# A bidirectional encoder block on one core: VectorE's order of work inside the RWKV-7 scan is changed

## The reference, cut to what matters

```python
k_dir = to_heads(k_raw[None] * (1.0 + (iclr - 1.0) * k_a[layer]))
wkv = rwkv7_bidir_scan(dir_stack(r_h, r_h), dir_stack(decay_h[0], decay_h[1]),
                       dir_stack(k_dir[0], k_dir[1]), dir_stack(v_h, v_h),
                       dir_stack(kk, kk), dir_stack(iclr_h[0], iclr_h[1]))
...
bonus = jnp.sum(jnp.sum(r_h[None] * k_dir * r_k[layer], axis=-1, keepdims=True) * v_h[None], axis=0)
o_rwkv = (gn + bonus.reshape(b, s, RWKV_WIDTH)) * gate
...
gates = jax.nn.sigmoid(z_gate.astype(f32).reshape(b, s, N_BRANCHES, D_MODEL) + b_gate[layer])
```

## Time and profile before

| | |
|---|---|
| median of 3 runs | 3952.27 us (3950.05 to 3955.77) |
| profiled execution | 3961.35 us, its span 3959.6 us |
| TensorE busy over the span | 3582.5 us (90%) |
| VectorE busy | 1654.8 us (42%) |
| scan, first `n_sb` to last | 1227.50 to 1979.56 us from the span's start |

### The profile page before, as it was taken

One profiled execution on the slowest core, in us unless ns is written; L12 is line 12 of the kernel. 1 busy time (PEld: TensorE's weight loads), 2 busy tenths in 40 slices (PEclk: granted clock), 3 DMA queues, 4 the chain that ended last, 5 costly groups with the idle time before them and its releaser, 6 DMA issues. The chain is left out here.

```text
span 3959.6 us, 45226 instructions
## 1 busy us (share of the span) xinstructions
PE 3582.5 (90%) x16478; PEld 2909.8 (73%) x16478; DVE 1654.8 (42%) x2026; ACT 1057.6 (27%) x1621; POOL 1627.8 (41%) x1347
## 2 busy tenths in 40 slices
PE   5999999886767899999957789999999999999999
PEld 4477788674545788888844668788888888888887
DVE  3066615663346677776614234432033213312321
ACT  4222211112322344444322222222122112212211
POOL 2033444331003766666633444344444344444443
PEclk9599999996558999999978889999999999999999
DMA  4333343331005545554323343332333333333323
GB/s 156 129 104 98 103 130 119 104 109 56 24 24 140 124 117 126 128 126 118 86 84 120 103 122 106 96 100 86 104 96 95 91 100 98 93 94 107 95 83 108
DMA packets 765541, 405.91 MB, mean 103 GB/s; under 512 B 191390, under 2 KB 726106, under 8 KB 764922
## 3 DMA queue, kind: packets, MB, share of 16 engines
q1 hardware_dynamic: 765434, 404.53, 35.5%
HBM read 345.73 MB, written 58.72 MB: 102 GB/s over the span
## 5 line engine op out<-in xcount | busy, mean ns | idle before, releaser
L131 POOL TENSOR_TENSOR w_lo_b<-w_raw_b,w_hi_b 128x2048 fp32r<-128x2048 f32 (+3 forms) x200 | 743.9, 3720 | 1012.4 <-ACT w_hi_b L124 1007.0
L140 PE MATMUL f_bank<-act_rounded,w_lo_b 128*128 128x512 f32 x1664 | 649.9, 391 | 22.7 <-POOL act_rounded L1896 14.9
L141 PE MATMUL f_bank<-act_rounded,w_hi_b 128*128 128x512 f32 x1664 | 648.9, 390 | 0.0
L142 PE MATMUL f_bank<-act_rounded,w_hi_b 128*128 128x512 f32 x1664 | 648.8, 390 | 0.0
L124 ACT CAST w_hi_b<-w_raw_b 128x2048 fp32r<-128x2048 f32 (+3 forms) x200 | 313.0, 1565 | 927.1 <-PE f_bank L142 862.5
L131 POOL TENSOR_TENSOR w_lo<-w_raw,w_hi 128x2048 fp32r<-128x2048 f32 x63 | 290.8, 4617 | 587.8 <-ACT w_hi L124 587.8
L140 PE MATMUL bank<-h_hi,w_lo 128*128 128x512 f32 x1008 | 405.5, 402 | 20.1 <-POOL w_lo L131 13.5
L141 PE MATMUL bank<-h_lo,w_hi 128*128 128x512 f32 x1008 | 396.2, 393 | 0.0
L142 PE MATMUL bank<-h_hi,w_hi 128*128 128x512 f32 x1008 | 396.2, 393 | 0.0
L140 PEld LDWEIGHTS f_bank<-act_rounded,w_lo_b 128*128 128x128 f32 x1664 | 313.4, 188 | 89.4 <-POOL act_rounded L1896 15.3
L141 PEld LDWEIGHTS f_bank<-act_rounded,w_hi_b 128*128 128x128 f32 x1664 | 313.5, 188 | 65.1
(11 more groups left out here) (319 smaller groups left out, 5373.7 us busy)
## 6 DMA issues: line engine op xcount, KB each, us to landing
w_raw<-in_w_in_dram SPq DMA_DIRECT2D x63, 1024.0 KB, 5.4
w_raw_b<-in_w_ffn_gate_dram SPq DMA_DIRECT2D x44, 1024.0 KB, 5.2
w_raw_b<-in_w_ffn_up_dram SPq DMA_DIRECT2D x44, 1024.0 KB, 5.1
w_raw_b<-in_w_ffn_down_dram SPq DMA_DIRECT2D x64, 704.0 KB, 4.4
gate_w_plain<-in_w_in_dram SPq DMA_DIRECT2D x64, 512.0 KB, 4.5
w_raw_b<-in_w_out_dram SPq DMA_DIRECT2D x16, 1024.0 KB, 5.7
zt<-out SPq DMA_DIRECT2D x60, 256.0 KB, 2.6
zt<-lout SPq DMA_DIRECT2D x40, 256.0 KB, 2.0
```

Source lines behind the costliest of these rows:

```text
L131: pool.tensor_tensor(g.w_lo[n.slot][:, 0:k, :], g.w_raw[n.slot][:, 0:k, :], g.w_hi[n.slot][:, 0:k, :].bitcast(F32), ALU.subtract).then_inc ...
L140: pe.matmul(bank, wl, hi[:, ka, :], start=start and j == 0, stop=False)
L141: pe.matmul(bank, wh, lo[:, ka, :], start=False, stop=False)
L142: ins = pe.matmul(bank, wh, hi[:, ka, :], start=False, stop=stop and j == len(ks) - 1)
```

## The change

VectorE's subtractions of a slot stand at other places of its list. `bonus_terms` moves from the middle of an odd slot (ahead of `decays`) to its end; the product with `head_ones` and `bonus_out` move one slot later, into the even slot c = 2b+2, and use the other bank, `gbank[1]`, which the gate slabs of odd slots use. SyncE's store and loads of the bonus move from the end of the even slot to the odd slot, behind the store of `n_sb`. `bonus_in(g, back)` gives the block whose odd slot lay `back` slots ago.

```diff
-def bonus_in(g):
-    return (g - 1) // 2 if g % 2 and (g - 1) // 2 < 2 * NPAIR else None
+def bonus_in(g, back):
+    b, even = divmod(g - back - 1, 2)
+    return b if not even and 0 <= b < 2 * NPAIR else None
...
+                    b = bonus_in(c, 2)
+                    if b is not None:
+                        sp.wait_ge(b_ready, b + 1)
+                        sp.dma_start(bonus_rows(b, ROW_BONUS), bonus[:, :]).then_inc(b_stored, 16)
+                    b = bonus_in(c, 0)
+                    if b is not None:
+                        for i, row in enumerate((ROW_RKV, ROW_RKV + RW, ROW_RKV + 2 * RW, ROW_IC, ROW_IC + RW)):
+                            sp.dma_start(b_in[:, i, :], bonus_rows(b, row)).then_inc(b_landed, 16)
                     if 1 <= c <= NGATE:
...
-                    if c % 2 == 0:
-                        b = c // 2
-                        if 1 <= b <= 2 * NPAIR:
-                            sp.wait_ge(b_ready, b)
-                            sp.dma_start(bonus_rows(b - 1, ROW_BONUS), bonus[:, :]).then_inc(b_stored, 16)
...
-                    dve.tensor_tensor(bonus[:, :], b_in[:, 2, :], gbank[0][:, 0:HS], ALU.mult).then_inc(b_ready, 1)
+                    dve.tensor_tensor(bonus[:, :], b_in[:, 2, :], gbank[1][:, 0:HS], ALU.mult).then_inc(b_ready, 1)
...
-                        if name == "decays" and bonus_in(c) is not None:
-                            bonus_terms(bonus_in(c))
-                        if name == "qg":
+                        if name == "xadd":
                             low_part(2 * c + 2, 1)
-                        if name == "operands":
-                            low_part(2 * c + 3, 0)
                         if name == "state":
-                            low_part(2 * c + 3, 1)
+                            low_part(2 * c + 3, 0)
...
-                    if bonus_in(c) is not None:
-                        bonus_out(bonus_in(c))
+                    low_part(2 * c + 3, 1)
+                    if bonus_in(c, 0) is not None:
+                        bonus_terms(bonus_in(c, 0))
+                    if bonus_in(c, 1) is not None:
+                        bonus_out(bonus_in(c, 1))
...
-                            if c % 2 == 0:
-                                pe.wait_ge(b_ready, c // 2)
+                            if c % 2:
+                                pe.wait_ge(b_ready, (c - 1) // 2)
...
-                        if name == "akv" and bonus_in(c) is not None:
-                            b = bonus_in(c)
+                        b = bonus_in(c, 1)
+                        if name == "akv" and b is not None:
                             pe.wait_ge(b_chain, 4 * b + 4)
                             pe.wait_ge(gate_taken, min(c, NGATE))
-                            pe.matmul(gbank[0][:, 0:HS], g.head_ones[:, :], b_in[:, 0, :], start=True, stop=True).then_inc(b_summed, 1)
+                            pe.matmul(gbank[1][:, 0:HS], g.head_ones[:, :], b_in[:, 0, :], start=True, stop=True).then_inc(b_summed, 1)
```

More of the change, by code:

```diff
@@ L889, in _ @@
                                      y_sb[:, :, :]).then_inc(y_stored, 16)
-                    if c % 2 == 0:
-                        b = c // 2
-                        if 1 <= b <= 2 * NPAIR:
-                            sp.wait_ge(b_ready, b)
-                            sp.dma_start(bonus_rows(b - 1, ROW_BONUS), bonus[:, :]).then_inc(b_stored, 16)
-                        if b < 2 * NPAIR:
-                            for i, row in enumerate((ROW_RKV, ROW_RKV + RW, ROW_RKV + 2 * RW, ROW_IC, ROW_IC + RW)):
-                                sp.dma_start(b_in[:, i, :], bonus_rows(b, row)).then_inc(b_landed, 16)
                 sp.wait_ge(y_stored, 16 * NUNIT)
@@ L1017, in _ @@
                         n = unit_at(slot, which)
-                        if name == "decays" and bonus_in(c) is not None:
-                            bonus_terms(bonus_in(c))
-                        if name == "qg":
+                        if name == "xadd":
                             low_part(2 * c + 2, 1)
-                        if name == "operands":
+                        if name == "state":
                             low_part(2 * c + 3, 0)
-                        if name == "state":
-                            low_part(2 * c + 3, 1)
                         if not has_stage(name, n):
```

## The result

| | before | after |
|---|---|---|
| median | 3951.16 us (4 runs, 3935.43 to 3955.77) | 3884.86 us (4 runs, 3877.64 to 3896.32) |
| profiled execution | 3961.35 us | 3877.64 us |
| first `n_sb` to last (S below) | 752.06 us | 683.05 us |

The changed kernel is 66.3 us faster by the medians. The ratio estimated from the runs is 0.9843 (62 us), with a 95% interval of 0.9814 to 0.9871 (51 to 73 us). The forecast was 3880 with a range of 3864 to 3908. The profiled execution of the kernel before is not one of its four. Further down, one of the ten executions of subs_only took 9889.72 us at a granted clock of 0.36 and is in no ratio.

The account below looks back on a forecast made before the run. TensorE bounds the scan but idles in odd slots behind VectorE's late bonus work, which also costs clock. 67.5 + 6.3 us, less 1.4 for `x3`, gives 72.4; about 72 off the median gives 3880 us, range 3864 to 3908.

Parts of the forecast that it names:

- What bounds the kernel: Scan: TensorE fills the even slots; 13 odd slots last 70.78 us more, from VectorE's lateness at `qg` and the clock.
- The terms leave the stretch ahead of `qg`: Odd slots: VectorE reaches `qg` early and waits for TensorE; slack of 2.19 us plus 0.7 covers slower scaling.
- The terms at the end of the odd slot: VectorE: terms take 2.2 us, `n_sb` about 1.6 us late, `xadd` 0.6 us to spare; 1.4 us lost in all.
- `bonus_out` and its product: Moved to the even slot: product costs TensorE 0.25 us; 1.2 us margin at the next odd slab's gate tile, no cost.
- SyncE: Bonus transfers issued 4 us later, behind the store of `n_sb`: VectorE's 37.4 us wait for loads vanishes.
- The start of the scan: Slots 1 to 4 shorten, but slot 5 waits for the first inversion: net 0, -3 to +3 us.
- The end of the scan: Last slots hang on the last inversion, which moves with `n_sb` of slot 32: all of the gain reaches the end.
- The sum: Scan: 67.5 us from odd slots 5 to 29, 6.3 from slot 31, less 1.4 for `x3`: 72.4 us gained.
- VectorE stays late: Rival: VectorE's work after `operands` runs at the slow rate, `xadd` 1.4 us late, 20 us given back, 3900; chance 0.12.
- GpSimd as the bound: Rival: denser VectorE work stretches the inversions past 43 us, so `x1` waits; about 3901; chance 0.06.
- the wait for `b_ready`: Rival: VectorE reaches `bonus_out` late, so TensorE stops at the head of odd slabs; slower, 3959; chance 0.04.
- no effect: Rival: the stall at `yh` has another cause, such as ScalarE's `u_bd`, and stays; about 3950; chance 0.02.

Follow-up runs that it names:

- subs_only: The kernel before with only the subtractions moved to their new places; ratio 0.9966 against the kernel before, S 724.36 us.
- bonus_only: The changed kernel with its subtractions back at their old places; ratio 0.9852 against the kernel before, S 681.01 us.
- no_terms: The changed kernel with a step that does nothing in place of the four bonus terms; one execution, 3890.03 us, S 680.93 us.
- late_load: The changed kernel with SyncE's bonus store and loads back at the even slot's end; ratio 0.9842 against the kernel before, S 683.06 us.
- dose2: The changed kernel with two more chained, unused products behind the bonus terms; one execution, 3899.68 us, S 691.15 us.
- dose5: The changed kernel with five more chained, unused products behind the bonus terms; one execution, 3902.72 us, S 709.16 us.
- early_load: The kernel before with SyncE's bonus store and loads moved up in the even slot, ahead of the second weights; ratio 0.9891 against it, S 704.98 us.
- terms_even: The changed kernel with the bonus terms in the even slot between `decays` and `qg`; ratio 0.9847 against the kernel before, S 680.12 us.

## Why the prediction was right, point by point

*What bounds the kernel.* Right: odd slots lost what VectorE's lateness at `qg` cost, and with it gone TensorE is busy in 605.4 of 606.7 us.

*The terms leave the stretch ahead of `qg`.* Right, and the single steps price it, by S: the late loads 47 us, the terms 24 (705.0 to 681.0, bonus_only), and the subtraction, tried first and alone, 28 (16 by the medians). The parts overlap, because each shortens the same stall. bonus_only shows that with the terms gone the subtraction ahead of `qg` costs nothing.

*The terms at the end of the odd slot.* The hand sum held to a few tenths: terms 2.2 forecast, 2.18 measured (2.1 to 2.4 in the slots 5 to 29); `n_sb` 1.6 late forecast, 1.96 measured; 0.6 us to spare ahead of `x3` forecast, 0.48 measured. The two doses show that this is the nearest wait. What the sum missed is the pairs of slots 5 and 6 and of slots 21 and 22. There TensorE's own work is 0.89 us shorter in a slot (21.46 against 22.35, since `yh` has no product with a state) and VectorE's is not, so the even slots stall: the pairs were 44.49 and 44.37 us where no_terms has 43.30 for each, 2.3 us together. The forecast took 1.4 us for all of the stalls at `x3`. It should have gone through the shortest slot too.

*`bonus_out` and its product.* Right in that there is no wait at the first gate tile of odd slots. The product's price was too low: 0.25 us was read from its start to the start of the next product, but that product is spread too (0.42 us to its successor, 0.23 otherwise), and in all 0.40 us of a slot goes (no_terms). The 13 pairs were forecast at 2 x 288.30 + 3.3 = 579.9 us; in no_terms they take 581.72, 1.8 us more.

*SyncE.* Right: late_load.

*The start of the scan.* The mechanism was right, the size was off: I took 2 us of gain, 5 us of waiting and up to 3 us through the clock. `x1` came 1.5 us earlier, waited 8.87 us, and the half clock then took what was gained: slots 1 to 4 are 0.3 us longer than before, against a net 0 forecast. The first inversion itself took 40.7 us instead of 38.7, beside a VectorE that was idle for 4.1 us of it instead of 10.3. Whether the one makes the other is not shown: in no_terms it took 40.5 us beside 6.6 us of idleness.

*The end of the scan.* Right: 1980.0 and 1979.6 us from the last `n_sb` to the end. The inversions of slots 6 to 28 took 39.0 to 39.5 us and ended 2 to 4 us into the even slot; "some 3 us" was forecast.

*The sum.* 72.4 forecast for the scan, 69.0 measured. The 3.4 us between them are the bonus' product (1.8), what the pairs took over those of no_terms (584.37 - 581.72 = 2.7 us, most of it in the two short pairs, 1.3 over the allowance) and the start (0.3). That the median came out as near to the forecast as 5 us is in part luck: 3884.86 lies between 3877.97 and 3891.76, and no execution took it. By the profiles, with the 14.2 us of the fast start added, the changed kernel took 3892 us where 3889 was forecast.

*The rivals.* VectorE stays late: no, though it was nearer than the prediction made it. The prediction leaned on a subtraction of 0.68 us with 3.5 us of the inversion left. In the changed kernel the one with 3.3 us left takes 0.88 us (the row at 1583.22) and only the next one 0.68, so GpSimd's tail is not free. Two more products of 0.5 us bring idleness to most `x3` (dose2), and five bring about this rival's price of 1.4 us a pair (dose5). GpSimd as the bound, the wait for `b_ready`, no effect: none showed.

## What to carry to other kernels

Cut a periodic phase into its periods and compare those that hold the suspect with those that don't: the plain period gave the floor (288.30 us) before any reason was known, and the forecast was little more than that number twice. When work is moved to a later place, add up the engine's list from the last point where it waits to the next wait of the bounding engine, at both prices that the trace shows, and do it for the period in which the bounding engine has least to do. And where a stall can cost clock, its price is not its length: in the profiled executions 1 us less of stall returned 1.9 us (subs_only) and 1.7 (early_load) in the odd slots. Such a price varies from execution to execution, so read it from the times of several too.

## What the runs showed that I had not expected

The prediction said that a stall of 3 us costs about 6 and one of 2 us costs 2, from two slots. The clock is less orderly. Slot 11 of the kernel before stood for 3.49 us (26.48 - 22.99) and kept its clock, the row below; slot 13 of subs_only, shown above, stood for 1.93 us and had a mean clock of 0.94.

```profile
1459.74:1486.22 26.48, 22.99 (x151) 20.32 (x150) 19.77 (x34) 10.39 (x24) 21.08 (x36) 1.00 0.53 135
```

In the kernel before all other odd slots from 5 to 29 with a stall of 3.07 us or more lost clock, and those with 1.84 to 2.63 us kept it. In subs_only slots 13 and 21 lost it at 1.93 and 2.51 us, while slots 15 and 17 kept it at 2.03 and 2.44. What decides it these runs don't show.

TensorE's clock ahead of 200 us is one source of scatter in this kernel's time: 194 products in a stretch where another execution starts 125, and 14 to 20 us of difference in the start of the scan (1213 against 1227 to 1233 us). Of the ten profiles three had the fast start (the changed kernel, bonus_only, dose5), and the changed kernel's own four times lie in two groups, 3877.6 and 3878.0, 3891.8 and 3896.3, as if the changed kernel had both kinds of start. It was not tried what sets it. It is not the only source: 30 executions of the kernel before spread over 43 us (3929.24 to 3972.21) and ten of early_load over 33, where four each of the changed kernel, bonus_only, late_load and terms_even spread over 5 to 20. Stalls that lose clock in one execution and not in the next would do that; with one profile of each kernel it is not shown.

With GpSimd beside it VectorE's chain of four terms took 2.77 us in mid-inversion (slot 19 before), 2.18 at the end, and 1.71 without it (from start to start), while instructions that read PSUM (`n_sb`, `qg`, `state`) stayed at 0.41 to 0.43 and 0.68 to 0.69 us throughout.
